# A head mixer whose units with 512 and with 256 keys run in turn instead of two by two

## The chip, the cores and the metric

The kernel runs on one core of a Trainium2 chip. The metric is the device time of one execution in microseconds. PE is TensorE, DVE is VectorE, ACT is ScalarE, SP is the engine that issues the weight loads.

## What is computed

Two transformer blocks follow each other, with two layers each. The change touches one stage: in the first layer of the second block, the attention part of the `even_mixer`. It has 8 heads of 64, 256 image tokens and 256 context tokens. Cut to what matters:

```python
def even_mixer(xm, cm, w_in, ...):
    u, va, q, k, vb = proj(xm)          # 256 image tokens
    uc, vac, qc, kc, vbc = proj(cm)     # 256 context tokens
    y_a = chunk_gmlp(u, va, ...)
    y_b = neighbourhood_attention(q, k, vb, kc, vbc, rpb)   # image queries: window with bias, and context
    y = concat([y_a, y_b]) @ w_out
    yc_a = chunk_gmlp(uc, vac, ...)
    yc_b = gqa_attend(qc, kc, vbc)                          # context queries: context keys only
    yc = concat([yc_a, yc_b]) @ w_out
```

Queries of the image see 512 keys (the image through a window with a bias, and the context). Queries of the context see the 256 context keys. Each row of scores goes through a softmax and is multiplied by the values. All is in float32.

## The kernel before

The kernel is a fixed list of stages (`plan`), and each engine walks through the same list with its own instructions, in the order in which they are written. Engines wait for each other by semaphores alone. An engine does nothing ahead of an instruction that waits.

The stage in question is `mix2` (`mix2_pe`, `mix2_dve`, `mix2_act`). A unit is one pair of heads i (0 to 3) with one block b of 128 queries (0 to 3); unit number 4i + b. Blocks 0 and 1 are image queries (512 keys), blocks 2 and 3 context queries (256 keys). The two heads of a unit are called c = 0 and 1. There are 16 units. For the unit at place t of the order:

- PE computes the scores into two banks of `PA` (L1412; for 512 keys also the bias, L1418), counted by `a2_s`. It waits for the exps of place t-2, which used the same banks (`a2_e`).
- DVE takes the two row maxima (L2161, `a2_m`) and, a step later, the reciprocals of the sums (L2168) and the scaling of the probabilities (L2170, `a_p`).
- ACT takes the two exps with their sums (L2742, `a2_e`).
- PE transposes the probabilities, 128 columns at a time, into banks 2 and 3 of `PB` (L1327, `a_T`). Each of the two halves waits until ACT has copied that half of the unit ahead of it (`a_ev`).
- ACT copies the transposes to SBUF (L2754, `a_ev`), into the tile `a_PT` of the unit's pair. The pair v is the units 2v and 2v+1, so both blocks of one kind for one pair of heads.
- PE multiplies by the values, for a whole pair at once (L1340, `a_o`); ACT and DVE split the result in a high and a low part (L2761, L2176, `a_hi`, `a_low`) for the output projection, which is the next stage (L917).

The three engines run in steps t = 0 to 19. In step t, PE has the scores of place t, the transposes of place t-2 and, for even t from 4 on, the value product of pair (t-4)/2. ACT has the exps of place t, the copies of place t-2, and in odd steps the high part of a pair. DVE has the maxima of place t, the scaling of place t-1, and in even steps the low part. In the first steps ACT and DVE also split the four tiles of the other half of the mixer (L2805, L2148). The same helpers (`attend_pe`, `attend`, `attend_act`) serve the later mixer `mix3`, where all units have 512 keys.

Of the kernel before, what the change touches and what calls it, by code (L numbers as in the profile page):

```python
# [134 lines left out]
def program(nc, hT, ctxT, params, lamv, wgate, wsb, rpb, c_both, c_first, c_second,  # L135
            w_in1, w_out1, w_gu1, w_dn1, w_ada, w_in2, w_out2, w_qkv, w_outc, w_up2, w_dn2, out):
    ctx = ExitStack()
    with ctx:
# [564 lines left out]
        def a_PT(second, j):  # L703

            at = ((8192, 0), (6144, 8192))[second][j]
            return [tiles(big, at + c * 1024, 4, 256) for c in range(2)]

        a_m, a_s, a_r = ([small[:, c + 2 * j:c + 2 * j + 2] for j in range(3)] for c in (21, 27, 40))

        g_mu = g_rt = big[:, 10752:11264]  # L710
# [114 lines left out]
        def _(pe):  # L825
# [487 lines left out]
                    spread_rows(o_bank(h), m1_row[0][:, 0:TQ], h).then_inc(S("o_bc"), 1)  # L1313
                ada_sums(B.first + 1, B.raw0 + 1)

            def attend_pe(second, n, scores, keys, value, beside):
                P0 = 16 * second

                def turn(p):
                    for c in range(2):  # L1320

                        pe.wait_ge(S("a_p"), 2 * (P0 + p) + c + 1)
                        if P0 + p:

                            pe.wait_ge(S("a_ev"), 2 * (P0 + p) + c - 1)
                        for kb in range(len(keys(p))):
                            mm = pe.transpose(PB[:, 2 + c, kb * 128:(kb + 1) * 128],  # L1327
                                              a_P[p % 3][c][:, kb * 128:(kb + 1) * 128], ident)
                        mm.then_inc(S("a_T"), 1)

                def values(v):

                    pe.wait_ge(S("a_ev"), 2 * P0 + 4 * v + 4)
                    if v >= 2:

                        pe.wait_ge(S("a_low"), P0 // 2 + v - 1)
                    blocks = keys(2 * v)
                    for j, kb in enumerate(blocks):
                        for c in range(2):
                            mm = pe.matmul(PB[64 * c:64 * c + 64, v % 2, 0:256], value(v, c, kb),  # L1340
                                           a_PT(second, v % 2)[c][:, j, :],
                                           start=(j == 0), stop=(j == len(blocks) - 1))
                    mm.then_inc(S("a_o"), 1)

                for t in range(n + 4):
                    if t < n:
                        scores(t)
                    if 2 <= t < n + 2:
                        turn(t - 2)
                    beside(t)  # L1350
                    if t >= 4 and t % 2 == 0:
                        values((t - 4) // 2)
# [41 lines left out]
            def mix2_pe(before):  # L1394

                pe.wait_ge(S("of_act"), before.a0 + before.n * before.outs)
                pe.wait_ge(S("v2_ev"), 4)
                pe.wait_ge(S("q2_ready"), 1)
                pe.wait_ge(S("bias_ready"), 1)

                def keys(p):
                    return range(4) if p % 4 < 2 else range(2, 4)

                def scores(p):
                    i, b = divmod(p, 4)
                    if p >= 2:

                        pe.wait_ge(S("a2_e"), 2 * p - 2)
                    k0 = 128 * keys(p)[0]
                    for c in range(2):  # L1410
                        r = slice(64 * c, 64 * c + 64)
                        mm = pe.matmul(PA[:, 2 * (p % 2) + c, 0:512 - k0], prj2[r, 8 + i, b * 128:(b + 1) * 128],  # L1412
                                       prj2[r, 12 + i, k0:512], start=True, stop=True)
                    if b < 2:
                        for c in range(2):
                            h = 2 * i + c

                            mm = pe.matmul(PA[:, 2 * (p % 2) + c, 0:SEQ], mirror,  # L1418
                                           Y[:, (2 * h + b) * 256:(2 * h + b + 1) * 256],
                                           start=False, stop=True, skip_group_check=True)  # L1420
                    mm.then_inc(S("a2_s"), 1)

                attend_pe(0, 16, scores, keys,
                          lambda v, c, kb: a_V[:, kb, (v // 2 * 2 + c) * 64:(v // 2 * 2 + c) * 64 + 64], lambda t: None)

            def rotate(n):
# [78 lines left out]
            def mix3_pe(before):  # L1505

                pe.wait_ge(S("of_act"), before.a0 + before.n * before.outs)
                pe.wait_ge(S("m3_ready"), 3)

                def last_values(t):  # L1510
                    if t == 0:
                        turn_heads(1)
                    elif t == 1:

                        pe.wait_ge(S("v3_ev"), 2)

                def scores(p):
                    j, b = divmod(p, 2)
                    if p == 2:
                        keep_busy(PB[:, 0, :], 5)  # L1520
                    if p >= 2:

                        pe.wait_ge(S("a3_e"), 2 * p - 2)
                    for c in range(2):
                        r = slice(64 * c, 64 * c + 64)
                        mm = pe.matmul(PA[:, 2 * (p % 2) + c, :], prj2[r, j, b * 128:(b + 1) * 128],  # L1526
                                       prj2[r, 8 + j // 4, :], start=True, stop=True)
                    mm.then_inc(S("a3_s"), 1)

                def value(v, c, kb):  # L1530
                    g = v // 4 * 2 + c
                    return m3_V[:, kb, g * 64:(g + 1) * 64]

                attend_pe(1, 16, scores, lambda p: range(4), value, last_values)


            pe.wait_ge(S("cboth_loaded"), 16)
# [20 lines left out]
        def _(dve):  # L1558
# [583 lines left out]
            def mix2_dve():  # L2142
                def gmlp_low(t):
                    if 2 <= t < 6:
                        g = t - 2

                        dve.wait_ge(S("g_hi"), g + 1)
                        dve.tensor_tensor(XL[:, g, :], prj2[:, 4 + g, :], XHf[:, g, :],  # L2148
                                          ALU.subtract).then_inc(S("g_ready"), 1)

                attend("a2", 0, 16, lambda p: 512 if p % 4 < 2 else 256, lambda v: (v // 2 + 4, v % 2 * 256), gmlp_low)

            def attend(name, P0, n, width, place, beside):
                def negmax(p):
# [129 lines left out]
        def _(act):  # L2284
# [369 lines left out]
            def mix1_act(l):  # L2654
# [75 lines left out]
                for h in range(4):  # L2730
                    act.wait_ge(S("o_n"), 4 * l + h + 1)
                    act.activation(XH[:, h, 0:T1], OB[:, h, :], ACT.Copy).then_inc(S("o_hi"), 1)
            def attend_act(name, P0, n, place, kbs, beside):
                def exps(p):

                    w = kbs(p) * 128
                    for c in range(2):
                        act.wait_ge(S(name + "_m"), 2 * p + c + 1)
                        if p >= 3:

                            act.wait_ge(S("a_T"), 2 * (P0 + p) + c - 5)
                        act.activation(a_P[p % 3][c][:, 0:w], PA[:, 2 * (p % 2) + c, 0:w], ACT.Exp,  # L2742
                                       bias=a_m[p % 3][:, c:c + 1],
                                       accum_out=a_s[p % 3][:, c:c + 1]).then_inc(S(name + "_e"), 1)

                def evac_T(p):
                    v = p // 2
                    for c in range(2):
                        act.wait_ge(S("a_T"), 2 * (P0 + p) + c + 1)
                        if v >= 2:  # L2750

                            act.wait_ge(S("a_o"), P0 // 2 + v - 1)
                        m = kbs(p)
                        act.activation(a_PT(P0 // 16, v % 2)[c][:, 0:m, (p % 2) * 128:(p % 2) * 128 + 128],  # L2754
                                       PB[:, 2 + c, 0:m * 128].rearrange("p (n t) -> p n t", t=128),
                                       ACT.Copy).then_inc(S("a_ev"), 1)

                def high(v):
                    k, col = place(v)
                    act.wait_ge(S("a_o"), P0 // 2 + v + 1)  # L2760
                    act.activation(XH[:, k, col:col + 256], PB[:, v % 2, 0:256], ACT.Copy).then_inc(S("a_hi"), 1)  # L2761

                for t in range(n + 4):
                    if t < n:
                        exps(t)
                    if 2 <= t < n + 2:
                        evac_T(t - 2)
                    if t >= 5 and t % 2 == 1:
                        high((t - 5) // 2)
                    beside(t)  # L2770
# [29 lines left out]
            def mix2_act():  # L2800
# [3 lines left out]
                        act.wait_ge(S("g_y"), t + 1)  # L2804
                        act.activation(XH[:, t, :], prj2[:, 4 + t, :], ACT.Copy).then_inc(S("g_hi"), 1)  # L2805

                attend_act("a2", 0, 16, lambda v: (v // 2 + 4, v % 2 * 256), lambda p: 4 if p % 4 < 2 else 2, gmlp_high)

            def head_squares(n):
                act.activation(m3_SQ[n], M3[n][0], ACT.Square).then_inc(S("m3_sq"), 1)  # L2810
# [35 lines left out]
            def mix3_act():  # L2846
                for n in range(2):
                    act.wait_ge(S("v3_T"), n + 1)
                    act.activation(m3_V[:, 2 * n:2 * n + 2, :], PB[:, 2 + n, :].rearrange("p (n c) -> p n c", c=256),
                                   ACT.Copy).then_inc(S("v3_ev"), 1)  # L2850
                attend_act("a3", 16, 16, lambda v: (v, 0), lambda p: 4, lambda t: None)

            before = None
            for idx, (what, x) in enumerate(plan):
# [139 lines left out]
```

## Time and profile before

| | us |
|---|---|
| median of 3 runs | 1693.38 |
| lowest and highest run | 1692.57, 1695.65 |
| the profiled execution | 1691.35 |
| its span, first to last instruction | 1689.6 |
| PE busy | 1616.5 |
| DVE busy | 1017.9 |
| ACT busy | 870.0 |
| the stage `mix2`, PE's first score matmul to its first projection matmul | 55.57 |

The span is what the profiler saw from the first to the last instruction of that one execution; the run's own time is 1.75 us longer. Busy times overlap, so they don't add up to the span. Matmuls are pipelined: a row's duration reaches a little over the start of the next row.

### The profile page before, as it was taken

What the parts mean: (1) busy time and instruction counts of PE and PEld (TensorE: products, weight loads), DVE (VectorE), ACT (ScalarE), POOL (GpSimd) and SP (SyncE); (2) the same over time, 40 slices, a digit from 0 to 9 for tenths busy, and PEclk for the clock granted to TensorE, in tenths of its full rate; (3) what the DMA queues carried; (4) which work ended last, traced back from release to release, by engine and by line L of the source; (5) the groups of instructions that cost most, each with busy time, mean ns of one, the idle gap of its engine ahead of it and who ended that gap; (6) DMA issues with size and microseconds to landing.
All of it is one profiled execution on the core that took longest, in us unless ns stands there. A gap on an engine that the chain in (4) does not pass through costs nothing.

```text
span 1689.6 us, 28191 instructions
## 1 busy us (share of the span) xinstructions
PE 1616.5 (96%) x11870; PEld 1407.3 (83%) x11870; DVE 1017.9 (60%) x1577; ACT 870.0 (51%) x1467; POOL 21.1 (1%) x38
## 2 busy tenths in 40 slices
PE   6999999999999999999989999999999898999997
PEld 6968999989789999987648777888888674789997
DVE  7675545465856555724555764424555777687585
ACT  6764534448545344544564543323444547766563
POOL 0000000000000000300000000000000000000000
PEclk9999999999999999999999999999999999999998
DMA  7465445354556464772202452232213530164642
GB/s 298 145 245 210 160 157 202 135 191 143 200 187 240 152 233 145 220 222 75 75 1 73 177 200 101 86 125 100 84 53 125 200 125 26 52 224 154 233 146 92
DMA packets 60524, 253.94 MB, mean 150 GB/s; under 512 B 4976, under 2 KB 8304, under 8 KB 42480
## 3 DMA queue, kind: packets, MB, share of 16 engines
q1 hardware_dynamic: 59088, 249.01, 41.6%
q0 software_dynamic: 1312, 3.15, 1.0%
q8 instruction: 94, 1.54, 0.4%
q14 instruction: 30, 0.25, 0.0%
HBM read 251.09 MB, written 1.05 MB: 149 GB/s over the span
## 4 chain that ended last, share of the span: by engine, by line
PE 81%; DVE 10%; ACT 6%; issue 2%; DMA 0%; SPq 0%; DVEq 0%; ACTq 0%
PE PA L917 63%; PE PA L977 3%; DVE W_t L1572 2%; PE PB L1340 2%; PE PB L852 2%; PE PA L1005 2%; ACT W_t L2299 1%; PE PB L1327 1%; PE PA L954 1%; PE PA L959 1%; PE PA L953 1%; PE PA L872 1%; PE PB L1270 1%; ACT tmp L2742 1%; PE PA L1412 1%
## 5 line engine op out<-in xcount | busy, mean ns | idle before, releaser
L917 PE MATMUL PA<-XH_t,W_t 128*128 128x256 f32 (+2 forms) x3968 | 873.3, 314 | 4.1 <-DVE W_t L1572 1.8
L917 PEld LDWEIGHTS PA<-XH_t,W_t 128*128 128x128 f32 x3968 | 650.1, 188 | 59.8 <-issue 6.0
L1572 DVE TENSOR_TENSOR W_t<-raw,W_t 128x1024 fp32r<-128x1024 f32 (+1 forms) x344 | 445.0, 1298 | 306.1 <-ACT W_t L2299 305.7
L917 PE MATMUL PA<-XL_t,W_t 128*128 128x256 f32 (+2 forms) x1984 | 620.5, 313 | 0.0
L2299 ACT ACTIVATE W_t<-raw 128x1024 fp32r<-128x1024 f32 (+1 forms) x344 | 381.4, 1113 | 155.6 <-PE PA L917 136.5
L917 PEld LDWEIGHTS PA<-XL_t,W_t 128*128 128x128 f32 x1984 | 373.1, 188 | 23.2 <-issue 0.5
L917 PE MATMUL PA<-AH_t,W_t 128*128 128x256 f32 (+2 forms) x1232 | 266.1, 311 | 0.2
L917 PEld LDWEIGHTS PA<-AH_t,W_t 128*128 128x128 f32 x1232 | 201.2, 188 | 14.1 <-DVE AL_t L1618 0.8
L917 PE MATMUL PA<-AL_t,W_t 128*128 128x256 f32 (+2 forms) x616 | 190.7, 310 | 0.0
L2457 ACT ACTIVATE tmp<-PA,par 128x512 f32<-128x512 f32 (+1 forms) x88 | 58.4, 667 | 133.0 <-PE PA L917 125.3
L1695 DVE SCALAR_TENSOR_TENSOR tmp<-PA,par,tmp 128x510 f32<-128x510 f32 (+1 forms) x88 | 53.6, 613 | 120.5 <-ACT tmp L2457 119.6
L917 PEld LDWEIGHTS PA<-AL_t,W_t 128*128 128x128 f32 x616 | 116.1, 188 | 6.7
L2412 ACT ACTIVATE big<-PA 128x272 f32<-128x272 f32 (+2 forms) x68 | 31.7, 466 | 118.0 <-PE PA L917 107.2
L977 PE MATMUL PA<-XH_t,W_t 128*128 128x256 f32 (+1 forms) x288 | 47.0, 294 | 8.2 <-DVE XL_t L1768 5.1
L2742 ACT ACTIVATE tmp<-PA,small 128x512 f32<-128x512 f32 (+1 forms) x64 | 40.2, 639 | 26.0 <-DVE small L2161 26.0
L2161 DVE TENSOR_REDUCE small<-PA 128x1 f32<-128x512 f32 (+1 forms) x64 | 36.8, 618 | 27.1 <-PE PA L1526 13.0
L852 PE MATMUL PB<-raw,cpad_t 128*32 128x256 f32 x768 | 52.3, 391 | 0.5 <-DMA raw<-in_w_ada 0.4
L977 PEld LDWEIGHTS PA<-XH_t,W_t 128*128 128x128 f32 x288 | 39.5, 193 | 14.8 <-issue 9.6
L1703 DVE SCALAR_TENSOR_TENSOR tmp<-PA,par,tmp 128x510 f32<-128x510 f32 (+1 forms) x88 | 50.1, 608 | 0.3
L1327 PEld LDWEIGHTS PB<-cboth,tmp 128*128 128x128 f32 x224 | 24.2, 140 | 30.7 <-DVE tmp L2170 23.1
L2444 ACT ACTIVATE tmp<-PA 128x272 f32<-128x272 f32 (+1 forms) x44 | 17.1, 390 | 62.2 <-PE PA L917 55.4
L977 PE MATMUL PA<-XL_t,W_t 128*128 128x256 f32 (+1 forms) x288 | 45.1, 289 | 3.1 <-DVE XL_t L1821 3.0
(275 smaller groups left out, 1576.4 us busy)
## 6 DMA issues: line engine op xcount, KB each, us to landing
raw<-in_w_ada SPq DMA_DIRECT2D x48, 1024.0 KB, 5.1
raw<-in_w_gu SPq DMA_DIRECT2D x44, 1024.0 KB, 4.8
raw<-in_w_dn SPq DMA_DIRECT2D x64, 704.0 KB, 4.0
raw<-in_w_up SPq DMA_DIRECT2D x44, 1024.0 KB, 4.8
raw<-in_w_in SPq DMA_DIRECT2D x30, 1024.0 KB, 5.5
raw<-in_w_out SPq DMA_DIRECT2D x12, 1024.0 KB, 4.8
raw<-in_w_qkv SPq DMA_DIRECT2D x6, 1024.0 KB, 6.3
raw<-in_w_outc SPq DMA_DIRECT2D x4, 1024.0 KB, 4.8
```

The costliest lines, as they stand in the source:

```text
L852: mm = pe.matmul(ada_psum[b // 6][0][32 * j:32 * j + 32, :], cpad[:, k, :], RAWV[:, r % RAW, c:c + 256], start=(k == 0), stop=(k == 7))
L917: mm = pe.matmul(PA[:, (L.b0 + o) % 4, 0:T], W[:, c:c + P], X[:, k, L.x0:L.x0 + T], start=(n == 0 and m == 0 and not L.early), stop=(n == ...
L977: pe.matmul(PA[:, bank % 4, a:b], WH_t[:, c:c + P], x[:, k, a:b], start=(k == 0 and x is hi), stop=False)
L1005: mm = pe.matmul(PA[:, bank % 4, a:b], WL_t[:, c:c + P], hi[:, k, a:b], start=False, stop=(k == KD - 1))
L1327: mm = pe.transpose(PB[:, 2 + c, kb * 128:(kb + 1) * 128], a_P[p % 3][c][:, kb * 128:(kb + 1) * 128], ident)
L1572: dve.tensor_tensor(WL_t[:, w:w + L.cols], RAWV[:, r % RAW, part * UNIT:part * UNIT + L.cols], WHf[:, w:w + L.cols], ALU.subtract).then_in ...
L1695: dve.scalar_tensor_tensor(c[:, :, 1:SEQ], ps[:, :, 0:SEQ - 1], tap(o, 0), c[:, :, 1:SEQ], ALU.mult, ALU.add).then_inc(S("conv_left"), 1)
L1703: dve.scalar_tensor_tensor(c[:, :, 0:SEQ - 1], ps[:, :, 1:SEQ], tap(o, 2), c[:, :, 0:SEQ - 1], ALU.mult, ALU.add).then_inc(S("of_dve"), 1)
L2161: dve.tensor_reduce(a_m[p % 3][:, c:c + 1], PA[:, 2 * (p % 2) + c, 0:width(p)], AX_X, ALU.max, negate=True).then_inc(S(name + "_m"), 1)
L2299: act.activation(WH_t[:, w:w + L.cols], RAWV[:, r % RAW, part * UNIT:part * UNIT + L.cols], ACT.Copy).then_inc(S("w_hi"), 1)
L2457: act.activation(conv[s % 2][x][:, 0:T], PA[:, (L.b0 + o) % 4, 0:T], ACT.Identity, bias=biasv(L.layer)[:, bass.ds(c, 1)], scale=tapv(L.lay ...
L2742: act.activation(a_P[p % 3][c][:, 0:w], PA[:, 2 * (p % 2) + c, 0:w], ACT.Exp, bias=a_m[p % 3][:, c:c + 1], accum_out=a_s[p % 3][:, c:c + 1 ...
```

## The change

The order of the units in `mix2` is no longer 0, 1, 2, 3 within a pair of heads but 0, 2, 1, 3, so that a unit with 512 keys and one with 256 keys take turns. The helper `woven` gives the unit at place t; `mix3` keeps its order through `straight`. The banks of `PA` and the buffers of the probabilities still go by the place. The pairs stay as they are, units 2v and 2v+1, and the value products keep their steps. So the value product of pair v waits for the copies of the last place that has a unit of the pair: of places 4i+2 and 4i+3, where it was 4i+1 and 4i+3.

```diff
+        def woven(t):
+            return t // 4 * 4 + (0, 2, 1, 3)[t % 4]
+
+        def straight(t):
+            return t
...
-            def attend_pe(second, n, scores, keys, value, beside):
+            def attend_pe(second, n, unit, scores, keys, value, beside):
...
-                        for kb in range(len(keys(p))):
+                        for kb in range(len(keys(unit(p)))):
...
-                    pe.wait_ge(S("a_ev"), 2 * P0 + 4 * v + 4)
+                    last = max(t for t in range(n) if unit(t) // 2 == v)
+                    pe.wait_ge(S("a_ev"), 2 * (P0 + last) + 2)
...
-                    i, b = divmod(p, 4)
+                    i, b = divmod(woven(p), 4)
...
-                    k0 = 128 * keys(p)[0]
+                    k0 = 128 * keys(woven(p))[0]
...
-                attend_pe(0, 16, scores, keys,
+                attend_pe(0, 16, woven, scores, keys,
...
-                attend("a2", 0, 16, lambda p: 512 if p % 4 < 2 else 256, lambda v: (v // 2 + 4, v % 2 * 256), gmlp_low)
+                attend("a2", 0, 16, lambda p: 512 if woven(p) % 4 < 2 else 256, lambda v: (v // 2 + 4, v % 2 * 256), gmlp_low)
...
-            def attend_act(name, P0, n, place, kbs, beside):
+            def attend_act(name, P0, n, unit, place, kbs, beside):
...
-                    v = p // 2
+                    v, half = divmod(unit(p), 2)
...
-                        act.activation(a_PT(P0 // 16, v % 2)[c][:, 0:m, (p % 2) * 128:(p % 2) * 128 + 128],
+                        act.activation(a_PT(P0 // 16, v % 2)[c][:, 0:m, half * 128:half * 128 + 128],
```

On PE, step 8 and the start of step 9, the scores at places 8 and 9 with what lies between them. Before, the scores of place 8 (512 keys), the transposes of place 6 (256 keys: two a half), the value product of pair 2 (512 keys: eight for each head) and the scores of place 9 (512 keys):

```order
L1412 MATMUL PA<-big 128x512 [waits a2_e]
L1412 MATMUL PA<-big 128x512
L1418 MATMUL PA<-Y,cphase 128x256 x2
L1327 MATMUL PB<-cboth,tmp 128x128 [waits a_ev,a_p]
L1327 MATMUL PB<-cboth,tmp 128x128
L1327 MATMUL PB<-cboth,tmp 128x128 [waits a_ev,a_p]
L1327 MATMUL PB<-cboth,tmp 128x128
L1340 MATMUL PB<-big,tmp 64x256 [waits a_low,a_ev]
L1340 MATMUL PB<-big,tmp 64x256 x7
L1412 MATMUL PA<-big 128x512 [waits a2_e]
L1412 MATMUL PA<-big 128x512
```

The same place on PE in the changed kernel (lines are 8 or 9 higher):

```order
L1421 MATMUL PA<-big 128x512 [waits a2_e]
L1421 MATMUL PA<-big 128x512
L1427 MATMUL PA<-Y,cphase 128x256 x2
L1335 MATMUL PB<-cboth,tmp 128x128 [waits a_ev,a_p]
L1335 MATMUL PB<-cboth,tmp 128x128 x3
L1335 MATMUL PB<-cboth,tmp 128x128 [waits a_ev,a_p]
L1335 MATMUL PB<-cboth,tmp 128x128 x3
L1349 MATMUL PB<-big,tmp 64x256 [waits a_low,a_ev]
L1349 MATMUL PB<-big,tmp 64x256 x7
L1421 MATMUL PA<-big 128x256 [waits a2_e]
L1421 MATMUL PA<-big 128x256
```

The value product stands where it stood. What is turned just ahead of it has 512 keys now, the scores behind it have 256, and its wait on `a_ev` is for the copies of the very unit turned just ahead.

On ACT, steps 8 to 11: the exps of a place and the copies of the place two before. Before:

```order
L2742 ACTIVATE tmp,small<-PA,small 128x512 [waits a_T,a2_m] x2
L2754 ACTIVATE big<-PB 128x2x128 [waits a_o,a_T] x2
L2742 ACTIVATE tmp,small<-PA,small 128x512 [waits a_T,a2_m] x2
L2754 ACTIVATE big<-PB 128x2x128 [waits a_o,a_T] x2
L2761 ACTIVATE XH_t<-PB 128x256 [waits a_o]
L2742 ACTIVATE tmp,small<-PA,small 128x256 [waits a_T,a2_m] x2
L2754 ACTIVATE big<-PB 128x4x128 [waits a_o,a_T] x2
```

In the changed kernel, from the same place:

```order
L2751 ACTIVATE tmp,small<-PA,small 128x512 [waits a_T,a2_m] x2
L2763 ACTIVATE big<-PB 128x4x128 [waits a_o,a_T] x2
L2751 ACTIVATE tmp,small<-PA,small 128x256 [waits a_T,a2_m] x2
L2763 ACTIVATE big<-PB 128x2x128 [waits a_o,a_T] x2
L2770 ACTIVATE XH_t<-PB 128x256 [waits a_o]
```

The exps of 512 keys now stand ahead of copies of 512 keys, those of 256 ahead of copies of 256, where the two kinds were crossed.

## Rows read from the trace of the kernel before

**Rows 1.** The page, part 4: shares of the chain that ended last.
```profile
PE 81%; DVE 10%; ACT 6%; issue 2%; DMA 0%; SPq 0%; DVEq 0%; ACTq 0%
```

**Rows 2.** Windows: length; PE, PEld, DVE, ACT, POOL busy; clock; DMA; GB/s.
```profile
831.07:886.64 55.57, 46.30 (x288) 27.06 (x288) 35.69 (x93) 38.85 (x111) 0.00 (x0) 1.00 0.06 20
```

**Rows 3.** Timeline of PE, 852 to 866: start, us, engine, line, operation, [idle before].
```profile
852.66 1.09 PE L1327 MATMUL PB<-cboth,tmp 128*128 128x128 f32 x8
853.68 1.13 PE L1412 MATMUL PA<-big 64*128 64x512 f32 x4
...
855.71 0.60 PE L1327 MATMUL PB<-cboth,tmp 128*128 128x128 f32 x4
856.24 1.95 PE L1340 MATMUL PB<-big,tmp 128*64 128x256 f32 x16
858.12 1.13 PE L1412 MATMUL PA<-big 64*128 64x512 f32 x4
...
860.67 0.70 PE L1412 MATMUL PA<-big 64*128 64x256 f32 x4
862.94 1.06 PE L1327 MATMUL PB<-cboth,tmp 128*128 128x128 f32 x8 [1.56 <-ACT big L2754]
863.93 1.08 PE L1340 MATMUL PB<-big,tmp 128*64 128x256 f32 x8
864.95 0.70 PE L1412 MATMUL PA<-big 64*128 64x256 f32 x4
865.58 0.66 PE L1327 MATMUL PB<-cboth,tmp 128*128 128x128 f32 x4
```

**Rows 4.** Timelines of all engines, DVE and ACT from 860 to 868.
```profile
860.35 1.29 DVE L2161 TENSOR_REDUCE small<-PA 128x1 f32<-128x512 f32 x2 [2.09 <-PE PA L1418]
...
861.07 0.69 ACT L2742 ACTIVATE tmp<-PA,small 128x512 f32<-128x512 f32 x1 [2.44 <-DVE small L2161]
...
862.41 0.66 ACT L2754 ACTIVATE big<-PB 128x256 f32<-128x256 f32 x2
...
863.39 0.88 DVE L2170 TENSOR_SCALAR tmp<-tmp,small 128x512 f32<-128x512 f32 x2
...
865.69 0.76 DVE L2161 TENSOR_REDUCE small<-PA 128x1 f32<-128x256 f32 x2 [1.09 <-PE PA L1412]
866.15 0.47 ACT L2742 ACTIVATE tmp<-PA,small 128x256 f32<-128x256 f32 x1 [0.93 <-DVE small L2161]
...
867.07 1.08 ACT L2754 ACTIVATE big<-PB 128x512 f32<-128x512 f32 x2
```

**Rows 5.** Groups by line and shape, 829 to 885: busy us, mean ns.
```profile
L2754 ACT ACTIVATE big<-PB 128x512 f32<-128x512 f32 x16 | 8.8, 615 | 0.0
```

**Rows 6.** Chain in order of time: between a copy and PE's next work.
```profile
862.80 0.14 issue
...
884.58 0.04 issue
```

**Rows 7.** Timeline of PE at places 2, 4 and 12 and at the end.
```profile
835.52 0.70 PE L1412 MATMUL PA<-big 64*128 64x256 f32 x4
...
840.76 1.13 PE L1412 MATMUL PA<-big 64*128 64x512 f32 x4
...
866.60 1.13 PE L1412 MATMUL PA<-big 64*128 64x512 f32 x4
...
883.43 0.66 PE L1327 MATMUL PB<-cboth,tmp 128*128 128x128 f32 x4
...
886.64 0.50 PE L917 MATMUL PA<-XH_t,W_t 128*128 128x512 f32 x1 [0.94 <-DVE XL_t L2176]
```

**Rows 8.** Chain in order of time, 884 to 1000: the output projection behind the stage.
```profile
886.64 44.58 PE PA L917 x192
```

**Rows 9.** A stretch with a lower clock: its window, and PE's timeline in it.
```profile
100.00:120.00 20.00, 18.65 (x167) 11.49 (x163) 14.37 (x67) 11.62 (x47) 0.00 (x0) 0.91 0.69 241
...
110.46 1.22 PE L1226 MATMUL PA<-big 64*128 64x256 f32 x4
```

More of the change, by code:

```diff
@@ L1532, in value @@
                     return m3_V[:, kb, g * 64:(g + 1) * 64]
-                attend_pe(1, 16, scores, lambda p: range(4), value, last_values)
+                attend_pe(1, 16, straight, scores, lambda p: range(4), value, last_values)
             pe.wait_ge(S("cboth_loaded"), 16)
@@ L2805, in gmlp_high @@
                         act.activation(XH[:, t, :], prj2[:, 4 + t, :], ACT.Copy).then_inc(S("g_hi"), 1)
-                attend_act("a2", 0, 16, lambda v: (v // 2 + 4, v % 2 * 256), lambda p: 4 if p % 4 < 2 else 2, gmlp_high)
+                attend_act("a2", 0, 16, woven, lambda v: (v // 2 + 4, v % 2 * 256), lambda p: 4 if woven(p) % 4 < 2 else 2, gmlp_high)
             def head_squares(n):
@@ L2850, in mix3_act @@
                                    ACT.Copy).then_inc(S("v3_ev"), 1)
-                attend_act("a3", 16, 16, lambda v: (v, 0), lambda p: 4, lambda t: None)
+                attend_act("a3", 16, 16, straight, lambda v: (v, 0), lambda p: 4, lambda t: None)
             before = None
```

## The prediction

> **What bounds the kernel now.** I read the page's chain first: PE holds 81% of what ended last, DMA nothing [rows 1]. Then the stretch of the head mixer that the change touches: 55.57 us, from PE's first score matmul at 831.07 to its first matmul of the output projection at 886.64, with PE busy for 46.30 of it at full clock [rows 2]. So only some 9 us of this stage are waiting, and only these can be won or added to. I call a unit's place in the order t, its scores s(t), its transposes turn(t), ACT's two copies of them evac(t), and the value product of pair v values(v). PE's timeline repeats every four units: s(4) starts at 840.76, s(8) at 853.68, s(12) at 866.60, 12.92 us apart [rows 3, 7]. The one real hole in a period, 1.56 us, lies ahead of turn(8), at 862.94, which waited for a copy by ACT [rows 3]. That copy, the first of evac(7), stands in ACT's list behind the exps of s(9), and these wait for DVE's maxima of s(9) [rows 4]: a round PE, DVE, ACT, PE. What the new order does to such rounds decides. Behind the stage PE works for 44.58 us without a hole [rows 8], so a later end of the stage is passed on in full.
>
> **Durations.** PE, from start to next start [rows 3]: scores of a 512-key unit with its bias 2.03 (855.71 less 853.68), of a 256-key unit 0.63 (865.58 less 864.95); transposes 1.02 for 512 keys (853.68 less 852.66) and 0.53 for 256 (856.24 less 855.71); values 1.88 (858.12 less 856.24) and 1.02 (864.95 less 863.93). From the start of a 512-key s to DVE's maxima 2.23 (860.35 less 858.12), to the exps another 0.72 (861.07), to ACT's next copy another 1.34 (862.41), since two exps lie between [rows 3, 4]. With 256 keys: maxima to exps 0.46, the two exps 0.92 [rows 4]. A pair of copies takes 1.08 for 512 keys, the first being done after about 0.62, and 0.66 for 256, the first after 0.39 (862.80 less 862.41) [rows 4 to 6]. From a copy's end to PE it is 0.14 for a transpose and 0.04 for a value product [rows 6].
>
> **The change part by part.** The work of each engine stays: the same 16 units, maxima, exps, copies and products, in another order; at the very end ACT's four 256-key copies become two of 512 keys and two of 256. So waits move the time, not work. (1) The hole ahead of turn(8) goes: s(9) has 256 keys now, its exps are done earlier, and PE comes to turn(8) later, behind a 512-key s(10). (2) A wait comes. A 512-key pair is now made of the places 4i and 4i+2, no longer 4i and 4i+1. values(2) stands in PE's list right behind turn(6), and needs evac(6), of what was only just turned. Before, it needed evac(5), and at 856.24 it started without idle time [rows 3]. The 256-key pairs (values(1), values(3)) still need what was turned a step earlier. Queued behind values(2) on PE are s(9), turn(7), s(10), and so the maxima on DVE and the exps on ACT. On ACT evac(6) stands behind the exps of s(8), so the new wait is a whole round.
>
> One period laid out by hand, zero at the start of s(8). s(8) to 2.03, turn(6) to 3.05. Maxima at 2.23, exps 2.95, evac(6) 4.29 to 5.37, values(2) at 5.41: **a hole of 2.36 us**. values(2) to 7.29, s(9) to 7.92, turn(7) to 8.45, s(10) to 10.48, turn(8) to 11.50. (turn(8) needs unit 8 scaled, which DVE does behind the maxima of s(9): these start at 8.03 and take 0.76, the scaling 0.88 [rows 4], a reciprocal between; done before 10.48.) values(3) to 12.52, s(11) to 13.15. turn(9) needs evac(8), behind the exps of s(10): 8.45 + 2.23 + 0.72 + 1.34 = 12.74; first copy done at 13.36, second at 13.82, so its two halves (0.27 each) start at 13.50 and 13.96, and s(12) at 14.23. Period 14.23 against 12.92, **+1.31**; twice, from s(4) to s(12), +2.62.
>
> The start: s(2) waits for the exps of s(0) as it does now, and starts at 835.52 [rows 7]. + 2.23 + 0.72 + 1.34 = 839.81 for evac(0), done at 840.89; + 0.14 + 0.27 gives s(4) at 841.30, for 840.76 [rows 7]: **+0.54**.
>
> The tail, zero at s(12), as above to turn(13), which ends at 14.23. The exps of s(15) follow evac(12) on ACT, 13.82 to 14.74, then evac(13) to 15.40. turn(14) starts at 14.74 + 0.39 + 0.14 = 15.27 and takes 1.02, being a 512-key unit now; its second copy can start when its last transpose is out, about 16.4, and takes 0.62; values(6) 17.05 to 18.93, a hole of 0.76. From the start of turn(15) to the projection it takes 3.21 as now (886.64 less 883.43), end 22.14, against 20.04 (886.64 less 866.60) [rows 7]: **+2.10**.
>
> Sum 0.54 + 2.62 + 2.10 = **+5.3 us**. It is made against the profiled execution, 1691.35 us with a span of 1689.6, which lies 2.0 below the median of the runs, 1693.38, and below all three (1692.57 to 1695.65). Put on the median it gives 1698.7, 0.31% more; on the profiled execution 1696.6. Within 0.2%, or 3.4 us, a measurement of this kernel can't tell a change from none.
>
> The new wait has no row of its own. From below: the round costs PE at least the present hole, 1.56, which is the same round with a 256-key unit of cover [rows 3]; that takes 0.8 off each of three holes and less off the tail, sum 2.7. From above: ACT is still late by one pair of copies, 0.66 [rows 4], in each of four, sum 7.9. I take the laid-out 2.36, since every link of it is in a row.
>
> PE's clock was granted in full in this stage [rows 2], with holes up to 1.56. In 100:120 it was granted at 0.91 on average, and there, after a run of very narrow matmuls, four matmuls of 64x256 took 1.22 us (half clock) where they take 0.70 here [rows 9, 3]. No row shows full clock across a hole of 2.4 us between such short bursts. The Trainium skill, "TensorE: Matmul & The Clock Gate", section "Why this matters for your kernels", warns against long idle gaps between bursts of matmuls, since they bring the clock back to half; by it rival B below would be the likelier the longer the hole, and no run here shows it for this one.
>
> **Rivals.** (A) The forecast, 1698.7. (B) The clock falls in the new holes too. One fall costs up to 1.8 us (0.09 of 20 us) [rows 9], so with one to four of them 1700.5 to 1705.9. For it: each hole follows nothing but transposes; against it: the present holes do no harm. (C) The new wait is covered and only the gain of alternation is left. Had evac(6) been done at the end of turn(6), three holes of 2.36 and one of 0.76, together 7.84, would be gone; the period would be 11.87, and the sum 5.3 - 7.8 = -2.5: 1690.9, not slower. It would need ACT to copy ahead of the exps, and its list has the exps of s(8) first. Holes of 0.8 instead of 2.36 are where it turns to no loss, and of 1.8 where the loss passes 0.2%. (D) The stage ends later, but a later wait for something with a pace of its own gives part of it back; half of it gives 1696.0, within 0.2%. Against it: DMA has 0% of the chain [rows 1], and DVE and ACT convert weights in list order behind this stage, so they shift with PE.
>
> **How the numbers follow.** A 0.80; B 0.07; C 0.05; D, or holes near their lower bound, 0.08. A alone spans 1696.8 to 1700.8, its holes off by 0.4 and the median by 0.5. Slower by over 0.2%: all of B and nearly all of A, 0.85. Faster by over 0.2% needs -3.4, which C doesn't reach by itself: 0.03. The same: 0.12. The range takes in D's half and the lower bound of the wait, and above the upper bound and one fall of the clock: 1696.0 to 1701.5.
>
> **What would show it.** PE idle for about 2.4 us ahead of values(0), values(2) and values(4), put down to ACT's copy, and 0.8 ahead of values(6); no hole of 1.56 ahead of turn(4), turn(8) and turn(12), but a few tenths ahead of turn(5), (9), (13); s(4), s(8) and s(12) 14.2 apart; the stage 60.9 long and all behind it as long as now. Wrong would be: a period near 11.9 (C), a granted clock under 1.00 in the stage (B), or a longer stage in an unchanged span (D).

## The result and the profile after

The changed kernel took 1701.29 us in the median of six runs (1698.49 to 1705.36), the kernel before beside it 1693.85 (six runs, 1691.65 to 1698.04). The ratio is 1.0049, 95% interval 1.0036 to 1.0062, so 0.49% slower, some 8 us. A second measurement on another occasion gave 1.0041 (1.0025 to 1.0057), some 7 us. The forecast was slower by 5.3 us, 0.31%, with a range up to 1701.5. The median lies just inside it. The ratio, put on the 1693.38 from which the forecast started, gives 1701.7, just outside. The direction was right and the size too small.

The profiled execution took 1700.57 us with a span of 1698.8, which is 9.2 more than the span before. Two windows of it follow, the whole stage from PE's first score matmul to its first projection matmul, and one period, s(8) to s(12). The columns are those of [rows 2].

```profile
832.11:894.86 62.75, 48.41 (x289) 27.77 (x289) 35.90 (x93) 38.68 (x111) 0.00 (x0) 0.97 0.05 18
...
856.81:871.20 14.39, 11.62 (x74) 6.80 (x73) 8.05 (x23) 8.43 (x27) 0.00 (x0) 1.00 0.01 1
```

The stage is 62.75 us long, for 55.57 before [rows 2]: 7.18 of the 9.2 are here. A period has 14.39 us for 12.92. And the granted clock of the stage is no longer 1.00.

PE's timeline from s(8) on answers to [rows 3]:

```profile
856.81 1.13 PE L1421 MATMUL PA<-big 64*128 64x512 f32 x4
...
858.83 1.04 PE L1335 MATMUL PB<-cboth,tmp 128*128 128x128 f32 x8
862.24 1.95 PE L1349 MATMUL PB<-big,tmp 128*64 128x256 f32 x16 [2.37 <-ACT big L2763]
864.12 0.70 PE L1421 MATMUL PA<-big 64*128 64x256 f32 x4
...
870.37 0.90 PE L1335 MATMUL PB<-cboth,tmp 128*128 128x128 f32 x4 [0.32 <-ACT big L2763]
871.20 1.13 PE L1421 MATMUL PA<-big 64*128 64x512 f32 x4
...
876.63 2.42 PE L1349 MATMUL PB<-big,tmp 128*64 128x256 f32 x16 [2.37 <-ACT big L2763]
878.98 1.22 PE L1421 MATMUL PA<-big 64*128 64x256 f32 x4
...
886.29 0.90 PE L1335 MATMUL PB<-cboth,tmp 128*128 128x128 f32 x4 [0.33 <-ACT big L2763]
...
889.77 1.95 PE L1349 MATMUL PB<-big,tmp 128*64 128x256 f32 x16 [0.74 <-ACT big L2763]
```

values(2) at 862.24 stands still for 2.37 us right behind its turn, and values(4) at 876.63 does again. The hole of 1.56 ahead of turn(8) is gone, turn(9) has a small one (0.32), and values(6) one of 0.74. But values(4) takes 2.42 for the same work that took 1.95 at 862.24, and s(13) takes 1.22 for its 0.70. The clock fell to half within values(4), right behind the hole: by the 0.47 that values(4) took longer, I estimate that its last 0.9 us ran at half clock, and so did s(13).

DVE and ACT on the round that ends in values(4) answer to [rows 4]:

```profile
873.42 1.29 DVE L2170 TENSOR_REDUCE small<-PA 128x1 f32<-128x512 f32 x2 [1.59 <-PE PA L1427]
...
874.15 0.69 ACT L2751 ACTIVATE tmp<-PA,small 128x512 f32<-128x512 f32 x1 [1.70 <-DVE small L2170]
...
875.49 1.08 ACT L2763 ACTIVATE big<-PB 128x512 f32<-128x512 f32 x2
```

ACT stood still for 1.70 us ahead of the exps, waiting for DVE's maxima, and at the end of it the first half of the transposes (873.22 on) was already out. It then did the two exps, and only then the copies that PE was waiting for. In the chain behind the stage PE has the same 44.58 us without a hole as in [rows 8]:

```profile
894.86 44.58 PE PA L925 x192
```

### The profile page after: what moved, and what is told of

Its sections match the earlier page's. It is cut to its first block, busy times and chain, and to the rows that moved or that the text cites. A ratio compares the mean times of both kernels' runs of the same rounds, so it can differ in the third digit from the quotient of the medians.

```text
span 1698.8 us, 28191 instructions
## 1 busy us (share of the span) xinstructions
PE 1621.7 (95%) x11870; PEld 1411.0 (83%) x11870; DVE 1018.5 (60%) x1577; ACT 871.0 (51%) x1467; POOL 21.1 (1%) x38
## 4 chain that ended last, share of the span: by engine, by line
PE 81%; DVE 10%; ACT 6%; issue 2%; DMA 0%; SPq 0%; DVEq 0%; ACTq 0%
PE PA L925 63%; PE PA L985 4%; DVE W_t L1581 2%; PE PA L1013 2%; PE PB L860 1%; PE PB L1349 1%; ACT W_t L2308 1%; PE PB L1335 1%; PE PA L962 1%; PE PA L967 1%; PE PA L961 1%; PE PA L880 1%; ACT tmp L2751 1%; ACT big L2763 1%; PE PA L1421 1%
```

## The experiments

Each was timed side by side with the kernel before, on several occasions, so that two experiments are best compared by their ratios. "Stage" is the stretch as above, from each kernel's own profile.

| kernel | median us | ratio to before (95%) | mean granted clock of the runs | stage us | falls of the clock in the stage |
|---|---|---|---|---|---|
| before | 1692.4 to 1693.9 | | 0.9923 | 55.57 | 0 |
| the change | 1701.29 | 1.0049 (1.0036 to 1.0062) | 0.9908 | 62.75 | 1 |
| woven_again | 1702.38 | 1.0041 (1.0025 to 1.0057) | 0.9912 | 62.83 | 1 |
| wait_only | 1706.64 | 1.0072 (1.0058 to 1.0087) | 0.9895 | 70.02 | 4 |
| woven_copy_first | 1695.53 | 1.0005 (0.9994 to 1.0016) | 0.9919 | 56.34 | 0 |
| woven_busy | 1702.44 | 1.0043 (1.0029 to 1.0057) | 0.9938 | 64.85 | 0 |
| woven_busy_5 | 1698.87 | 1.0033 (1.0021 to 1.0045) | 0.9942 | 61.30 | 0 |
| straight_copy_first | 1690.50 | 0.9987 (0.9978 to 0.9997) | 0.9924 | 52.25 | 0 |
| straight_late | 1688.94 | 0.9982 (0.9974 to 0.9991) | 0.9935 | 52.06 | 0 |
| straight_late_copy_first | 1686.38 | 0.9962 (0.9949 to 0.9974) | 0.9933 | 49.16 | 0 |
| woven_late_copy_first | 1689.23 | 0.9977 (0.9966 to 0.9988) | 0.9932 | 51.98 | 0 |
| both_mixers | 1678.17 | 0.9907 (0.9894 to 0.9921) | 0.9942 | 49.17 | 0 |

The clock of before is the mean over the 17 runs beside woven_again, wait_only, woven_copy_first and woven_busy; beside woven_busy_5 and the three straight ones it was 0.9937, beside the last two 0.9929. A fall is a short stretch at half clock; those counted are in the one profiled execution of each kernel, and only in the stage.

**The change once more.** No edit.

> The changed kernel once more, beside the others on one chip. Wait theory (the value product of each 512-key pair waits a whole round, four times): about 5.3 to 5.7 us of the stage above the kernel before, by the hand layout. Clock theory: on top of that some falls of PE's clock to half in the new holes, 1 to 3 us in sum, with a mean granted clock below that of the kernel before, and single runs that are slower the lower their clock. Together 1699 to 1702.

1702.38 us, 0.4 above the expected range; as a ratio, 7 us more than before. The profile shows the same holes, and again one fall of the clock, but at another hole: values(2) took 3.07 us at 860.49, where in the first profile values(4) was the slow one.

**The wait alone, in the old order.**

```diff
-                    pe.wait_ge(S("a_ev"), 2 * P0 + 4 * v + 4)
+                    pe.wait_ge(S("a_ev"), 2 * P0 + 4 * v + (6 if not second and v % 2 == 0 else 4))
```

> The old order, with nothing but the wait: the value product of each even pair also waits for the copies of the unit turned just ahead of it. The result needs no such wait, so the kernel computes the same. Wait theory: holes of about 2.4 us ahead of values(0), (2), (4), some 0.6 ahead of values(6), the stage 7.8 us longer than before, time 1701 to 1704, since the old hole of 1.56 stays too. Rival (the loss comes from the new order, exps and copies of one width side by side, and the wait only shows it): below +1 us, under 1695.

PE's timeline of this kernel, its four late value products and one of the old holes, ahead of turn(4):

```profile
844.54 2.99 PE L1340 MATMUL PB<-big,tmp 128*64 128x256 f32 x16 [2.37 <-ACT big L2754]
...
852.88 1.06 PE L1327 MATMUL PB<-cboth,tmp 128*128 128x128 f32 x8 [1.56 <-ACT big L2754]
...
861.54 2.93 PE L1340 MATMUL PB<-big,tmp 128*64 128x256 f32 x16 [2.38 <-ACT big L2754]
...
878.55 2.87 PE L1340 MATMUL PB<-big,tmp 128*64 128x256 f32 x16 [2.38 <-ACT big L2754]
...
893.13 3.59 PE L1340 MATMUL PB<-big,tmp 128*64 128x256 f32 x16 [0.47 <-ACT big L2754]
```

The hole of 2.37 is there in the old order too, so it belongs to the wait and not to the order of the units. The old hole of 1.56 stays beside it. And each of these value products takes 2.9 to 3.6 us where it took 1.95: the clock fell at every one of them. The profiled stage was 14.45 us longer than before, of which the holes explain 7.6 (3 x 2.37 + 0.47), and the four falls nearly all of the rest: the stage's granted clock was 0.90, and a tenth of 70.02 is 7.0. The price of a fall can be read from a period: turn(4) at 852.88 to turn(8) at 869.88 is 17.00, while 12.92 + 2.37 would be 15.29, so a fall costs 1.7 us here. The median of the runs, 13.2 above before (1706.64 less 1693.46), is more than the waits alone could give, and 2.6 above the expected 1701 to 1704, which had counted the waits alone.

**The new order, with copies ahead of the exps in every fourth step.**

```diff
+                    first = name == "a2" and t % 4 == 0
+                    if first and 2 <= t < n + 2:
+                        evac_T(t - 2)
                     if t < n:
                         exps(t)
-                    if 2 <= t < n + 2:
+                    if not first and 2 <= t < n + 2:
                         evac_T(t - 2)
```

> The new order, but in ACT's steps 0, 4, 8, 12, 16 the copies of the unit just turned stand ahead of the exps. Wait theory: the hole ahead of values(0), (2), (4) shrinks from 2.37 to about 0.7 us, a period is near 12.7, the stage 55.5 to 56.5 long; time 1693.5 to 1695, the same as before. Rival (delayed exps cost as much as the wait gave, since the maxima of the next units queue behind): 1698 or more.

```profile
859.94 1.09 ACT L2763 ACTIVATE big<-PB 128x512 f32<-128x512 f32 x2 [1.41 <-PE PB L1335]
...
860.91 0.69 ACT L2751 ACTIVATE tmp<-PA,small 128x512 f32<-128x512 f32 x1
...
861.08 1.95 PE L1349 MATMUL PB<-big,tmp 128*64 128x256 f32 x16 [0.74 <-ACT big L2763]
```

ACT takes the copies as soon as the transposes are out, the exps come behind, and values(2) stands still for 0.74 in place of 2.37. The stage is back at 56.34 and the time is that of the kernel before: 1.0005. The three holes are 1.63 shorter each, 4.9 together, which with the fall of 1.5 is the 6.4 between 62.75 and 56.34. So the hole carries the loss. The median lies 0.5 above the expected range, the stage inside its own. That is rival C's condition, brought about by hand, in part.

**Does the clock add to it?** The new order with throw-away matmuls in the hole, first eight in each long hole and three in the short one, then five and one (the wait on `a_low` moves ahead of them):

```diff
+                    if not second and v % 2 == 0:
+                        keep_busy(PB[:, v % 2, 256:512], 3 if v == 6 else 8)
                     pe.wait_ge(S("a_ev"), 2 * (P0 + last) + 2)
```

> The new order, with eight matmuls whose result is thrown away in the hole ahead of values(0), (2), (4) and three ahead of values(6). They fit in the hole, so the layout of the stage stays as long as in the changed kernel at full clock (62 us or a little less). Clock theory: no fall of the clock in the stage, a mean granted clock like that of the kernel before, 1698.5 to 1699.5, 1 to 3 us faster than the changed kernel. Rival (all of the loss is waiting, the clock plays no part): the same time as the changed kernel.

The eight took longer than the hole, so the expected 1698.5 to 1699.5 was missed: the stage became 64.85 us. The clock stayed full in it. Beside it, on the same occasion, woven_again took 1702.38 with a granted clock of 0.9912 against 0.9938 here. By its stage woven_busy should be 3.6 us slower than the changed kernel at full clock (64.85 less the 61.30 below), and it was not slower than the real one, 1702.44. That speaks for falls in the runs of the changed kernel, though medians of six runs that spread by 5 to 7 us give no exact price.

> As woven_busy, with five thrown-away matmuls in each of the three long holes and one in the short one. Eight took longer than the hole and stretched a period from 14.39 to 15.40 us; one takes about 0.42, so five (2.1) end inside 2.37. Clock theory: the stage at 61.2 us with no fall in it, a mean granted clock at or above that of the kernel before, time 1698 to 1699.5, so 2 to 3 us under the changed kernel. Rival (the clock plays no part): 1701 to 1702.

```profile
858.38 2.32 PE L870 MATMUL PB<-cboth 128*128 128x256 f32 x10
860.91 1.95 PE L1351 MATMUL PB<-big,tmp 128*64 128x256 f32 x16 [0.21 <-ACT big L2765]
...
830.78:892.08 61.30, 53.80 (x320) 32.85 (x320) 35.90 (x93) 38.67 (x111) 0.00 (x0) 1.00 0.05 18
```

Five fill all but 0.21 us of the hole (L870, a matmul counts as two records). The value product starts when it did, so the order has its full price, and there is no fall: the stage takes 61.30 us at full clock. The runs' mean granted clock is 0.9942, against 0.9908 and 0.9912 in the two measurements without them, and the median 1698.87 lies 2.4 and 3.5 us under those of 1701.29 and 1702.38. These were not timed side by side, and on its occasion the kernel before had a higher clock too (0.9937 for 0.9923) and was 0.9 us faster. As ratios it is 1.0033 (1.0021 to 1.0045) against 1.0049 and 1.0041, and the intervals overlap. The profiles show the falls and their price; that they make 1 to 3 us of the median is likely, and not settled by the times alone.

**The old order with cures for its own rounds.** Copies first in every step; value products (with high and low parts) one step later; and both:

```diff
-                    if t >= 4 and t % 2 == 0:
-                        values((t - 4) // 2)
+                    if v0 <= t < v0 + n and (t - v0) % 2 == 0:
+                        values((t - v0) // 2)
```

Here `v0` is 5 for this mixer, 6 on ACT and 7 on DVE.

> The old order, with ACT's copies ahead of its exps in every step. If the rounds PE, DVE, ACT, PE set the stage, the hole of 1.56 ahead of turn(4), (8), (12) falls to about 0.9 and the one ahead of turn(14) shrinks; by the hand layout the stage is 3.6 us shorter than before, time 1689.5 to 1690.5. Rival (exps that come later delay PE as much): 1693 or more.

> The old order, with each value product (and its high and low parts) one step later. The product of 1.0 us then lies ahead of the late turn and no longer behind it, so it covers the hole: 0.56 instead of 1.56 three times; by the hand layout 3.6 us shorter, 1689.5 to 1690.5. Rival (a product that stands later delays the projection at the end by its own length): 1693 or more.

> Both of the two others together. By the hand layout the stage is 6.3 us shorter than before, about 49.3, with PE nearly without holes from place 4 on; time 1686.5 to 1688. Rival (both cover the same hole, so that they don't add up): 1689.5 to 1690.5.

The stages took 52.25, 52.06 and 49.16 us, so 3.3, 3.5 and 6.4 less than before. The medians follow: 1690.50 at the upper end of its expected range, 1688.94 and 1686.38 a little under theirs. The two cures nearly add up, though both work on the same hole, the 1.56 ahead of turn(4), (8) and (12): copies first leave 0.91 of it (which then waits for DVE's scaling), the later product leaves 0.51, and both together leave none. In the kernel with both, PE stands still for more than 0.3 us four times only, at the start of the stage and at its end:

```profile
834.09 1.13 PE L1413 MATMUL PA<-big 64*128 64x512 f32 x4 [0.69 <-ACT big L2413]
...
840.37 1.09 PE L1327 MATMUL PB<-cboth,tmp 128*128 128x128 f32 x8 [1.13 <-DVE tmp L2171]
...
878.86 0.70 PE L1327 MATMUL PB<-cboth,tmp 128*128 128x128 f32 x4 [1.00 <-DVE tmp L2171]
...
883.25 0.50 PE L917 MATMUL PA<-XH_t,W_t 128*128 128x512 f32 x1 [0.94 <-DVE XL_t L2177]
```

**The new order with both cures.** As above, with the value products of the 512-key pairs alone one step later.

> The new order with both cures: ACT's copies ahead of its exps, and the value product of the 512-key pairs one step later, so that it no longer stands right behind the turn that it needs. By the hand layout the stage is 3.6 us shorter than before, 1689 to 1691; the same cures in the old order give 6.3. If alternation itself were of use once its wait is gone, this would beat the old order with both cures (1686.4).

1689.23 us with a stage of 51.98, for 1686.38 and 49.16 in the old order. With its wait cured, taking turns still isn't ahead. The holes left are at its start, where s(2) waits 1.63 us behind a short s(1), in each period, where the turn ahead of a 512-key product waits 0.34 for DVE's scaling (a period is 11.77 us for 11.32), and at its end, where the last turn of 512 keys stands.

**Both cures in the later mixer too**, the same edit for `mix3`.

> The old order with both cures in this mixer and in the later one too, where PE stands still before a turn for ACT's copies five times for 0.77 us and once for 1.83, 6.4 us in all. If the same round bounds that mixer, 3 to 6 us less than with the cures in this mixer alone: 1681 to 1683.5. Rival (there the later value product delays the projection behind it by as much): 1685 to 1687.

1678.17 us, 0.9907 (0.9894 to 0.9921): 14 us faster than before and the best version found. It beat its expectation by 3 to 5 us. What PE waits for in the later mixer, all of it:

```profile
PE PB L1327 <- DVE tmp L2171: 0.4, 1, 0.4
PE PA L1527 <- ACT tmp L2743: 0.3, 1, 0.3
PE PA L1527 <- ACT big L2413: 0.2, 1, 0.2
```

The holes of 6.4 us that the expectation counted are gone (six of 0.77 and one of 1.83; "five" was a miscount, the sum is right), and one of 0.7 ahead of the last value product with them. From its first score matmul to the projection the later mixer takes 52.28 us (1390.34 to 1442.62) for 59.79 (1396.58 to 1456.37) before, 7.5 less; the medians of the kernels with the cures in one mixer and in both are 8.2 apart, from two occasions. The expectation took only 3 to 6 of it; the cost at the end that its rival feared didn't come.

## Why the prediction fell short

- **The new wait.** Right in place and size: 2.36 was worked out, 2.37 measured, three times; 0.76 and 0.74 ahead of values(6). wait_only shows that it comes with the wait alone, woven_copy_first that without most of it the loss is gone.
- **The hole that goes.** Right: none ahead of turn(4), (8), (12).
- **The period.** 14.23 worked out, 14.39 measured, so two give +2.94 where the sum has +2.62. turn(9) takes 0.83 from its first half to s(12) (871.20 less 870.37), where I had 0.73, and begins 0.06 later than laid out.
- **The stage at full clock.** 60.9 forecast, 61.30 in woven_busy_5, the profile with no fall: +5.7 where the sum said +5.3. The start was forecast at +0.54 and measured +0.62 in the profile after (s(4) at 842.42, 10.31 behind the start; 9.69 before), and the tail, without the fall, is the +2.10 of the sum.
- **The clock. This step failed.** The forecast of +5.3 put nothing for the clock, and the prediction set rival B at 0.07, since "the present holes do no harm". The new hole, 2.37 us behind a short run of transposes, brought the clock to half at one of three long holes in each of two profiles. In wait_only it fell at all four holes, the last of them only 0.47 long behind one of 1.13. A fall costs 1.5 to 1.7 us: in the profile after, turn(9) to turn(13) took 15.92 (886.29 less 870.37), where the period is 14.39. The Trainium skill, "TensorE: Matmul & The Clock Gate", section "Why this matters for your kernels", warns against idle gaps between bursts; it was cited and then priced as a mere rival. The gaps that it warns of are longer than these, and the traces show falls at the shorter ones too.
- **Why the premise was weak.** That the present holes do no harm was read from one profile. The later mixer, which none of these kernels but both_mixers changes, has one hole of 1.83 us behind transposes. PE's timeline there, first in the kernel before, then in straight_copy_first:

```profile
1449.74 1.11 PE L1327 MATMUL PB<-cboth,tmp 128*128 128x128 f32 x8 [1.83 <-ACT big L2754]
1450.79 1.95 PE L1340 MATMUL PB<-big,tmp 128*64 128x256 f32 x16
...
1444.89 1.92 PE L1327 MATMUL PB<-cboth,tmp 128*128 128x128 f32 x8 [1.83 <-ACT big L2754]
1446.73 2.72 PE L1340 MATMUL PB<-big,tmp 128*64 128x256 f32 x16
```

The same hole brought no fall in the first and one in the second. In the eleven profiles that have this hole the clock fell at it in three (woven_copy_first, straight_copy_first, woven_late_copy_first). So one profile with full clock doesn't show that a hole is harmless.
- **The sum.** 5.7 for the layout and one fall of 1.5 make the 7.2 of the profiled stage. The other 2 us of the profile's 9.2 are outside the stage, where the two kernels have the same work: 1.04 ahead of it and 0.98 behind it (803.94 us from its end to the end of the span, for 802.96). There too the clock had fallen where it hadn't in the profile before: it was 0.91 in 150:170 and 0.95 in 1310:1345, and 1.00 in both before. The profile of woven_again has neither, so these two vary from one execution to the next. The medians, 7 to 8 us, fit the layout and one or two falls. How many falls the other runs had isn't on record, only their mean granted clock.
- **Rivals C and D.** C needed holes of 0.8 for no loss by its working; woven_copy_first has holes of 0.74, and measured 1.0005. D is out: behind the stage PE had its 44.58 us without a hole, and the stretch from there to the end was no shorter than before in the profile after, and only 0.4 shorter in that of woven_again (802.60).
- **The range.** Its upper end of 1701.5 had room for the upper bound of the wait (7.9) or for one fall of the clock, but not for both together, though both come from the same holes.

## What to carry over

When units are reordered in a pipeline of several engines, look for each product at which unit it now needs last, and how many instructions stand between that unit and the product in the waiting engine's list: a product right behind the work whose copy it needs waits a whole round over all engines. Put the work that another engine waits for (a copy) ahead of the work that waits for that engine (the exps), and give a consumer one step more of distance: each was worth 3.3 to 3.5 us of the stage here, and with both in place the one other order that was tried was slower than the old. A hole on TensorE can have a second price, since the clock may fall in it; a forecast that adds holes should add that too. No run here gives the chance: behind holes of the same 2.37 us the clock fell at one of three or at three of three, behind the same 1.83 in three profiles of eleven.

## What the runs showed that was not expected

- Runs of one kernel spread by 5 to 7 us, and their time goes with the granted clock: before, 1691.3 us at 0.994 and 1697.0 at 0.990. As an estimate, 0.004 of 1690 us is 6.8, so the clock alone is enough for the 5.7 between them.
- Five throw-away matmuls of 256 columns took 2.3 us in the hole and held the clock in the profile, with the 512-key product behind them no later; the very last value product of the stage waited 0.62 for 0.53.
